# Sums of squares over heads as two float32r products of rounded parts, in a dilated-attention stage

## What is computed

```python
def rms_norm(x, g):
    x32 = x.astype(jnp.float32)
    y = x32 * lax.rsqrt(jnp.mean(x32 * x32, axis=-1, keepdims=True) + EPS)
    return (y * g.astype(jnp.float32)).astype(x.dtype)
...
def dilated_attention_branch(h, cos, sin, w_in, q_norm, k_norm, w_out):
    B, S, _ = h.shape
    u = h @ w_in
    q, k, v, gate = jnp.split(u, [QKV_DIM, 2 * QKV_DIM, 3 * QKV_DIM], axis=-1)
    shp = (B, S, N_GROUPS, HEADS_PER_GROUP, HEAD_DIM)
    q = partial_rope(rms_norm(q.reshape(shp), q_norm), cos, sin)
    k = partial_rope(rms_norm(k.reshape(shp), k_norm), cos, sin)
    v = v.reshape(shp)
    ...
```

## Time and profile before

| what | us |
| --- | --- |
| median of 3 runs | 1782.96 (1782.12 to 1783.45) |
| the profiled execution, its time | 1783.8 |
| the profiled execution, its span | 1781.4 |
| TensorE busy | 1759.5 (99%) |
| VectorE busy | 1138.1 (64%) |
| ScalarE busy | 1167.9 (66%) |
| GpSimd busy | 315.3 (18%) |

### The profile page before, as it was taken

The page is one execution under the profiler, slowest core; times in us unless marked ns, Lnnn a source line. Parts: engine busy times, 40 slices in busy tenths (PEclk is TensorE's granted clock), DMA queues, the critical chain, the costliest instruction groups (busy, mean ns, idle before and its releaser), DMA issues.

```text
span 1781.4 us, 26641 instructions
## 1 busy us (share of the span) xinstructions
PE 1759.5 (99%) x10285; PEld 1456.3 (82%) x10285; DVE 1138.1 (64%) x1946; ACT 1167.9 (66%) x1730; POOL 315.3 (18%) x409
## 2 busy tenths in 40 slices
PE   8999999999999999999999999999999999999999
PEld 6788678777787887989989876767777879899897
DVE  6999668756647677727537465696754477275372
ACT  6677768667667676746647675666675567466473
POOL 1122111322322111111111111001110111111111
PEclk9999999999999999999999999999999999999999
DMA  8798698765665687787787976545656887878777
GB/s 247 184 213 204 173 236 205 170 159 133 157 153 134 158 202 183 185 188 185 194 188 178 257 191 155 119 112 131 148 130 165 204 190 182 202 173 192 193 174 182
DMA packets 93644, 317.54 MB, mean 178 GB/s; under 512 B 12368, under 2 KB 12496, under 8 KB 92752
## 3 DMA queue, kind: packets, MB, share of 16 engines
q0 software_dynamic: 47440, 148.93, 44.2%
q1 hardware_dynamic: 43488, 156.00, 27.5%
q10 hardware_dynamic: 2592, 10.94, 1.7%
HBM read 160.88 MB, written 6.29 MB: 94 GB/s over the span
## 4 chain that ended last, share of the span: by engine, by line
PE 77%; DVE 13%; ACT 5%; DMA 3%; issue 2%; ACTq 0%; DVEq 0%
PE ps L2133 45%; PE ps L2243 18%; DVE cv_acc L1679 3%; DVE tmp L1679 3%; PE ps L2150 3%; DMA w_lo<-w_raw 2%; PE ps L2208 2%; ACT w_hi L615 1%; PE ps L2471 1%; PE ps L2483 1%; ACT w_lo L629 1%; PE ps L2726 1%; PE ps L2687 1%; PE ps L2512 1%; PE ps L2771 1%
## 5 line engine op out<-in xcount | busy, mean ns | idle before, releaser
L550 POOL DMA_DIRECT2D w_lo<-w_raw x289 | 249.9, 865 | 1346.0 <-ACT w_lo L629 1265.4
L615 ACT ACTIVATE w_hi<-w_raw 128x1024 fp32r<-128x1024 f32 (+1 forms) x289 | 288.6, 999 | 139.7 <-PE ps L2133 122.6
L2133 PE MATMUL ps<-H_hi,w_hi 128*128 128x512 f32 x680 | 278.4, 409 | 4.7 <-DMA w_lo<-w_raw 4.7
L2133 PE MATMUL ps<-H_hi,w_lo 128*128 128x512 f32 x680 | 265.7, 391 | 0.0
L2133 PE MATMUL ps<-H_lo,w_hi 128*128 128x512 f32 x680 | 265.6, 391 | 0.0
L629 ACT ACTIVATE w_lo<-w_raw 128x1024 fp32r<-128x1024 f32 x253 | 264.8, 1047 | 0.0
L2133 PEld LDWEIGHTS ps<-H_hi,w_hi 128*128 128x128 f32 x680 | 128.0, 188 | 40.4 <-issue 9.5
L1365 DVE SCALAR_TENSOR_TENSOR X<-ps,X 128x512 f32<-128x512 f32 (+1 forms) x68 | 49.2, 723 | 174.1 <-PE ps L2133 166.2
L2133 PEld LDWEIGHTS ps<-H_lo,w_hi 128*128 128x128 f32 x680 | 128.2, 188 | 32.0 <-issue 6.5
L2133 PEld LDWEIGHTS ps<-H_hi,w_lo 128*128 128x128 f32 x680 | 128.0, 188 | 27.3
L2133 PE MATMUL ps<-mid_hi,w_hi 128*128 128x512 f32 x352 | 137.2, 390 | 1.5 <-DVE mid_lo L1372 1.5
(11 more groups left out here) (426 smaller groups left out, 4061.7 us busy)
## 6 DMA issues: line engine op xcount, KB each, us to landing
w_raw<-weights SPq DMA_DIRECT2D x289, 512.0 KB, 4.3
w_lo<-w_raw POOLq DMA_DIRECT2D x253, 512.0 KB, 5.3
w_lo<-w_raw POOLq DMA_DIRECT2D x36, 256.0 KB, 4.7
cv_yl<-cv_a POOLq DMA_DIRECT2D x8, 256.0 KB, 3.3
pl_P<-spill ACTq DMA_DIRECT2D x1, 2048.0 KB, 9.7
spill<-X ACTq DMA_DIRECT2D x8, 256.0 KB, 6.7
X<-spill ACTq DMA_DIRECT2D x2, 1024.0 KB, 6.4
out<-X SPq DMA_DIRECT2D x8, 256.0 KB, 3.8
```

The costliest lines, as they stand in the source:

```text
L550: pool.dma_start(w_lo[:, u, 0:width], w_raw[:, u, 0:width], accum_op=ALU.add).then_inc(lo_landed[u], 16)
L615: return act.activation(out_ap, in_ap, ACT.Copy)
L2133: mm = pe.matmul(ps[:, bank, :], w, x, start=first and n == 0 and q == 0, stop=last and n == len(blocks) - 1 and q == 2, skip_group_check= ...
```

## The change

The squares are split in two float32r parts, and the sum is made as two float32r products, which accumulate in the same bank. The constant matrix is copied once into a float32r tile `at_ones`. ScalarE writes the high part `at_qh` (one buffer) in its slot j + 1, behind `guess_var` of the tile before. VectorE subtracts it from the squares in its slot j + 1, behind `masked_pair` and ahead of `head_newton`, and writes the low part `sq_r`, which lies over `sq`. TensorE waits for the low part where it waited for the squares.

```diff
@@ tiles
+        sq_r, = scope(("sq_r", [P, 2, S], F32R))
         sq = sb("sq", [P, 2, S])
...
+                ("at_qh", [P, S], F32R), ("at_ones", [P, P], F32R))
@@ ScalarE, for c in range(4), for j in range(SLOTS)
                     if c == 0 and j == 0:
                         prep()
+                        copy(at_ones[:, :], head_ones)
                         logs()
                         guess(4, 1.0 / D)
                     if j - 1 in SUM_SLOT:
                         k.up(sq_used)
                         guess_var()
+                    if j in SUM_SLOT:
+                        act.wait_ge(sq_done, k.at(sq_done))
+                        copy(at_qh[:, :], sq[:, (k.n[sq_done] - 1) % 2, :]).then_inc(square_hi, 1)
@@ VectorE, the same loops
                         head_var(1)
                     if pair is not None:
                         masked_pair(*pair)
+                    if j in SUM_SLOT:
+                        n = len(QK_TILES) * c + SUM_SLOT[j]
+                        dve.wait_ge(square_hi, n + 1)
+                        dve.tensor_tensor(sq_r[:, n % 2, :], sq[:, n % 2, :], at_qh[:, :].bitcast(F32), ALU.subtract)\
+                            .then_inc(square_lo, 1)
                     prep()
@@ TensorE, the same loops
-                        sum_squares(0, 1, 1, head_ones)
+                        pe.wait_ge(square_lo, n + 1)
+                        pe.matmul(ps[:, 1, :], at_ones[:, :], at_qh[:, :], start=True, stop=False)
+                        pe.matmul(ps[:, 1, :], at_ones[:, :], sq_r[:, n % 2, :], start=False, stop=True).then_inc(sq_used, 1)
+                        k.up(sq_done)
+                        k.up(sq_used)
```

More of the change, by code:

```diff
@@ L230, in build @@
                                 ("rp", [P, 5, S], F32))
-            (at_raw, at_pair, at_mask, at_T, at_SG, at_Sm, at_PT, at_Yh, at_Yl, at_V, at_st) = scope(
+            (at_raw, at_pair, at_mask, at_T, at_SG, at_Sm, at_PT, at_Yh, at_Yl, at_V, at_st,
+             at_qh, at_ones) = scope(
                 ("at_raw", [P, 12, S], F32), ("at_pair", [P, 2, S], F32), ("at_mask", [P, 4, S], F32),
@@ L234, in build @@
                 ("at_Sm", [P, 2, S], F32), ("at_PT", [P, 2, PT_COLUMNS], F32),
-                ("at_Yh", [P, 4, S], F32R), ("at_Yl", [P, 4, S], F32R), ("at_V", [P, 6, S], F32), ("at_st", [P, 4, 4], F32))
+                ("at_Yh", [P, 4, S], F32R), ("at_Yl", [P, 4, S], F32R), ("at_V", [P, 6, S], F32), ("at_st", [P, 4, 4], F32),
+                ("at_qh", [P, S], F32R), ("at_ones", [P, P], F32R))
         mid_hi, mid_lo, B_hi, B_lo, w_sum, s_hi, s_lo = scope(
@@ L284, in build @@
         sq_used = sem("sq_used")
+        square_hi = sem("square_hi")
+        square_lo = sem("square_lo")
         r0_done = sem("r0_done")
```

## The result

The changed kernel takes 1795.55 us (median of 6 runs, 1790.95 to 1796.79); the kernel before, beside it, 1783.24. The ratio is 1.0061, with a 95% interval of 1.0048 to 1.0075: slower by 0.6%, some 11 us by the ratio and 12.3 by the medians. The forecast was 1791.7, in a range of 1786 to 1799. The profiled execution has a span of 1794.8, which is 13.4 above that of the profile before.

A forecast was written before the change was run, and what follows sets the result against it. TensorE was taken to bound the kernel except in attention's chunk 0, set by VectorE, which has half a microsecond to spare in two later slots. Chunk 0 +6.6 and three later chunks +2.1 give +8.7: 1791.7 us, range 1786 to 1799.

The forecast's parts named there:

- V to V: VectorE, start of one variance to the next: even slots grow from 7.08 to 8.23 us, odd ones to 9.42.
- The two products: TensorE, each sum of squares: two float32r products take 0.455 us instead of 0.86, saving 0.40 a sum.
- First sum of the stage: Chunk 0: the first sum waits for the subtraction behind the stage's statistics and starts at 316.4 instead of 314.12.
- before the sums of slots 4 to 6: Chunk 0: TensorE waits about 2.3 us for VectorE before each of these sums.
- waits before the transposes: Chunks 1 to 3: TensorE waits for the probabilities in slots 3 and 5, 0.7 and 2.3 us.
- Chunk to chunk: Each of chunks 1 to 3: +1.1 us inside the chunk less 0.40, so +0.7; three chunks +2.1.
- Chunk 0 at the first scores: First scores of chunk 0 come 6.6 us later, 359.31 becoming 365.9.
- The clock: Rival: the six tiles of chunk 0 at half rate, 33 us more, 1825; chance 0.01.
- The weights of slot 7: ScalarE's weight preparation moves up to about 2.6 us later against at least 3.1 of cover: costs nothing.
- Faster: Rival: copy and subtraction find room and TensorE keeps 24 x 0.40, 1773.3; needs even slots under 7.3 us; chance 0.07.
- No change: Rival: chunk 0 loses 6.6 us, later chunks keep 18 x 0.40 = 7.2, giving 1782.4; chance 0.10.
- Much slower: Rival: VectorE's lag never closes and sets slots 2 to 7 in each chunk, 1801; chance 0.10.

The follow-up runs named there:

- e7: The changed kernel run again, with no edit: 1794.36 us, ratio 1.0057 to the kernel before.
- e9: Second run of the changed kernel with ScalarE's preparation of slot 7's weights moved ahead of the guess and table loads: 1796.33 us, ratio 1.0062 to the kernel before.
- e3: The changed kernel with ScalarE's preparation of slot 7's weights moved ahead of the guess and table loads: 1793.84 us, ratio 1.0059 to the kernel before.
- e8: The changed kernel with six extra TensorE products ahead of the wait for the low part in slots 4 to 6 of chunk 0: 1794.40 us.
- e2: The changed kernel with ScalarE's copy of the high part ahead of the guess instead of behind it: 1781.68 us, ratio 0.9982 to the kernel before.
- e1: The changed kernel without the low part: no subtraction, the sum one float32r product of the high part: 1774.36 us, ratio 0.9944 to the kernel before.
- e10: The changed kernel with ScalarE's copy ahead of the guess and the split only in chunks 1 to 3: 1779.34 us, ratio 0.9970 to the kernel before.
- e11: As e10, but slots 3 and 5 of chunks 1 to 3 also keep the float32 product: 1779.23 us, ratio 0.9971 to the kernel before.
- e5: The changed kernel with the subtraction made by GpSimd instead of VectorE, copy still behind the guess: 1825.29 us, ratio 1.0231 to the kernel before.

## Why the prediction was right

**The mechanism** was as forecast, step by step. V to V: 8.20 for a forecast of 8.23, odd slots 9.32 for 9.42. The two products: 0.46 for 0.455. First sum of the stage behind the statistics. Waits of 2.0 to 2.1 before the sums of slots 4 to 6, forecast 2.3. In the later chunks waits before the transposes of 0.62 and 2.12, forecast 0.7 and 2.3, and none before a sum. Chunk to chunk 75.47 against 74.87, +0.6 for a forecast of +0.7. Chunk 0 at the first scores: in e7's trace its next tile starts 57.36 behind the stage's start against 50.85, +6.5 for a forecast of +6.6. The trace of e9 has one fall of the clock (1.2 us) and no late weights: its stage is 9.5 longer than before, so 8.3 without the fall, for a forecast of 8.7.

**The size** was 2 to 5 us short: +8.7 forecast, +11 by the ratio, +13.4 in the profile. In the profile after, two terms that I had put at nothing or among the rivals made the rest, 1.2 and 3.6 us.
- *The clock.* The rival had all six tiles of chunk 0 at half rate, with a chance of 0.01. What happens is milder and frequent: a fall that slows TensorE for 6 to 8 products behind one wait. In the profile after it cost 1.2 in chunk 0; in e7 and e3 some 1.5 in each of chunks 1 and 2, in e8 1.6 in chunk 1. All five traces of kernels with this order have at least one in the stage. Where VectorE sets the time, as at 344 to 352 in e7, a fall costs nothing. I had argued against it from one window of the kernel before that stayed at 1.00. That row was true of its execution only: in e1, the window behind it, 188 to 192, has 0.76.
- *The weights of slot 7.* "Cost nothing" rested on the cover of the tile that this transfer serves. That tile was in time. But the landing of this low part also releases SyncE's next load, and that load then ran beside the low part of slot 8, whose user at the end of chunk 3 has no slot to spare. It cost 0.9 us (e8, 39.78 from V7 to the end of the stage) to 1.9 (e7, 40.79) against the 38.9 of e3 and e9, and 3.6 in the profile after, where the clock fell behind the wait. The step that failed is the one that asked only who waits for the late transfer, and not what its landing starts.

**The rivals.** Faster: its condition (an even slot under 7.3) is met by e2 from slot 4 of chunk 0 on, and there the kernel is faster, if only by 2 to 3 us, because the odd slots still grow (9.17 for 8.46). No change: the later chunks kept nothing of the 7.2 us, each became 0.6 longer. Much slower: S6 waited for the transposes of slot 5 and not for the subtraction, so the lag closed in each chunk.

## What to carry to other kernels

Work moved off the busiest engine is free only if it falls into a wait of the engines that take it, so look at the order as well as the load: here the change costs 11 us with ScalarE's copy behind the guess and saves 2 to 3 with it ahead. Where VectorE sets the time (chunk 0) the split gains nothing and cost 1.3 us in e2; where VectorE has no wait (odd slots) it gained next to nothing (e10 against e11). If a loop's engines are within a few per cent of each other in length, a gain on one is bounded by the slack of the next (in e10 5.1 us of a possible 7.2, from 18 sums). When a transfer gets later, ask what its landing releases, not only who needs it.

## What the runs showed of the hardware

- The granted clock falls behind some waits of TensorE of about 2 us, in some executions and not in others, and at different waits: 352 and 604 in the profile after, 344, 420 and 500 in e7, 316 and 420 in e8, 316, 356, 424 and 500 in e3, 352 alone in e9. These are 12 of the 32 waits of 1.6 to 2.2 us that the stages of the five traces have. A fall makes products start 0.43 apart instead of 0.23 and costs 1.2 to 1.7 us if TensorE sets the time there. Even ahead of the changed stage it comes and goes. The same window in the kernel before and in e1:

```profile
188.00:192.00 4.00, 3.82 (x9) 1.29 (x9) 3.14 (x6) 2.53 (x5) 0.00 (x0) 1.00 1.07 253
```
```profile
188.00:192.00 4.00, 3.20 (x6) 1.30 (x6) 3.75 (x7) 2.46 (x5) 0.00 (x0) 0.76 1.06 254
```

It may make up part of the spread of 6 us among the runs of the changed kernel: the mean granted clock is 0.998 in the fastest of them and 0.995 to 0.997 in the others. The page "TensorE: Matmul & The Clock Gate" of the Trainium skill, section "What's actually happening", says that the clock goes to its lower level, 1.2 GHz, after idleness. The traces agree in that these 12 falls stand behind waits; behind the 20 other waits of that length there is none.

- A subtraction by GpSimd of two 128x512 operands in SBUF stretched VectorE's two-operand instruction beside it from 0.69 to 2.60 us (e5). The Trainium skill, "SBUF — State Buffer", section "Summary: rules for kernel authors", says that where VectorE has two inputs in SBUF and GpSimd reads SBUF, the second to issue is fully blocked until the first is done. The trace agrees in that VectorE's instruction ends 0.57 us behind GpSimd's, but here the one stretched is the one that the trace has starting first (344.74 against 345.20).
